# Causal masks of three forgetting pairs written into the forget terms instead of added by matmuls

## What is computed

```python
cum = lax.cumsum(log_f, axis=2)                       # one term for each head and position
logits = einsum('bhqd,bhkd->bhqk', qb, k) * scale
logits = logits + cum_q[..., :, None] - cum[..., None, :]
causal = key_pos[None, :] <= q_pos[:, None]
p = softmax(where(causal, logits, -inf), axis=-1)
out = einsum('bhqk,bhkd->bhqd', p, v)
```

## Time and profile before

| | |
|---|---|
| runs | 756.1 us median of 3 (752.18 to 759.27) |
| profiled execution | 752.78 us |
| its span, first to last instruction | 751.0 us |
| mean granted TensorE clock | 0.988 |
| TensorE busy | 704.8 us, 94% |
| VectorE busy | 490.6 us, 65% |
| ScalarE busy | 425.1 us, 57% |
| GpSimd busy | 363.0 us, 48% |

### The profile page before, as it was taken

How to read it: one execution, slowest core, us unless ns; L and a number is a source line. 1 busy time by engine, 2 the same in 40 slices (tenths; PEclk the granted TensorE clock), 3 DMA queues, 4 the chain that set the end, 5 groups by cost and what they waited for, 6 DMA issues and landing times.

```text
span 751.0 us, 10774 instructions
## 1 busy us (share of the span) xinstructions
PE 704.8 (94%) x3830; PEld 587.1 (78%) x3830; DVE 490.6 (65%) x994; ACT 425.1 (57%) x884; POOL 363.0 (48%) x300
## 2 busy tenths in 40 slices
PE   2989979899999989999999999999989999999995
PEld 0667867788888878888887788888878887888884
DVE  4977997746655776566558764655686654555566
ACT  5875656655675645566756464666565665323222
POOL 1010462466885545688757355866574653321100
PEclk9999999999999999999999999999999998999998
DMA  9932230233442110234420102445312087792222
GB/s 353 409 140 85 92 127 7 86 98 113 139 152 95 38 57 0 99 113 142 168 101 26 42 1 85 154 166 169 101 49 85 22 281 237 231 301 85 85 113 112
DMA packets 35463, 93.14 MB, mean 124 GB/s; under 512 B 4297, under 2 KB 5961, under 8 KB 34898
## 3 DMA queue, kind: packets, MB, share of 16 engines
q1 hardware_dynamic: 28450, 73.71, 28.3%
q0 software_dynamic: 5376, 14.68, 6.1%
q10 hardware_dynamic: 1584, 4.05, 1.4%
HBM read 68.81 MB, written 23.63 MB: 123 GB/s over the span
## 4 chain that ended last, share of the span: by engine, by line
PE 79%; ACT 8%; DVE 8%; issue 3%; POOL 2%; DMA 0%; DVEq 0%; ACTq 0%; POOLq 0%
PE psum L1643 12%; PE psum L1550 12%; PE psum L1552 11%; PE psum L1551 11%; PE psum L1631 8%; PE psum L1607 7%; PE psum L1576 4%; PE psum L1575 4%; DVE work L1203 2%; DVE stacks L1171 2%; PE psum L1480 1%; ACT work L891 1%; ACT work L892 1%; PE psum L1481 1%; PE psum L1494 1%
## 5 line engine op out<-in xcount | busy, mean ns | idle before, releaser
L1550 PE MATMUL psum<-h_hi,w_hi 128*128 128x512 f32 x448 | 186.4, 416 | 5.1 <-DVE stacks L1171 5.1
L1552 PE MATMUL psum<-h_hi,w_lo 128*128 128x512 f32 x448 | 176.5, 394 | 0.0
L1551 PE MATMUL psum<-h_lo,w_hi 128*128 128x512 f32 x448 | 175.4, 391 | 0.0
L686 POOL TENSOR_TENSOR work<-work 128x127 f32<-128x127 f32 (+3 forms) x64 | 80.1, 1252 | 173.3 <-DVE work L1203 173.3
L931 ACT ACTIVATE pt_hi<-psum 128x512 fp32r<-128x512 f32 (+1 forms) x192 | 87.8, 490 | 105.4 <-PE psum L1607 102.3
L1264 DVE TENSOR_TENSOR pt_lo<-psum,pt_hi 128x512 fp32r<-128x512 f32 (+1 forms) x192 | 101.0, 553 | 54.7 <-ACT pt_hi L931 52.4
L1203 DVE TENSOR_TENSOR_SCAN work<-work 128x128 f32<-128x128 f32 (+3 forms) x64 | 100.4, 1569 | 37.9 <-ACT work L892 37.7
L1550 PEld LDWEIGHTS psum<-h_hi,w_hi 128*128 128x128 f32 x448 | 85.3, 190 | 20.6 <-issue 6.5
L1552 PEld LDWEIGHTS psum<-h_hi,w_lo 128*128 128x128 f32 x448 | 84.5, 189 | 19.5
L1551 PEld LDWEIGHTS psum<-h_lo,w_hi 128*128 128x128 f32 x448 | 85.2, 190 | 14.7
L1607 PE MATMUL psum<-ident,work 128*128 128x128 f32 x576 | 88.5, 281 | 8.6 <-POOL work L686 8.0
(11 more groups left out here) (185 smaller groups left out, 1325.1 us busy)
## 6 DMA issues: line engine op xcount, KB each, us to landing
w_raw<-in_w_blocks SPq DMA_DIRECT2D x30, 512.0 KB, 4.3
w_split_scratch<-work SPq DMA_DIRECT2D x16, 512.0 KB, 3.2
work<-in_x SPq DMA_DIRECT2D x12, 512.0 KB, 7.3
work<-in_w_ada_t SPq DMA_DIRECT2D x10, 512.0 KB, 6.4
y_split_scratch<-work SPq DMA_DIRECT2D x10, 512.0 KB, 3.6
v_stack_early<-in_w_ada_t SPq DMA_DIRECT2D x8, 512.0 KB, 3.4
work<-forget_scratch SPq DMA_DIRECT2D x8, 512.0 KB, 5.1
work<-in_w_out SPq DMA_DIRECT2D x16, 256.0 KB, 3.3
```

The source lines that it names most:

```text
L1550: nc.tensor.matmul(bank, hi, h_hi[:, c_, cols], start=(c_ == 0), stop=False)
L1551: nc.tensor.matmul(bank, hi, h_lo[:, c_, cols], start=False, stop=False)
L1552: last = nc.tensor.matmul(bank, lo, h_hi[:, c_, cols], start=False, stop=(c_ == DC - 1))
```

## The change

In pairs 1, 3 and 5 the mask matmul at L1579 is left out. The mask goes into `CUM[a]` instead: GpSimd writes -1e30 above the diagonal into each of its eight 128-column blocks by one affine select in place. A unit needs its diagonal block masked and the blocks before it unmasked, so as soon as a unit is past its maximum, the block that was its diagonal one is loaded again from `c_dram`, unmasked, by a transfer that ScalarE issues behind the exponential (64 KB, none after the last unit of a head). VectorE waits for the select ahead of a head's first unit, and for the transfer ahead of each later one. GpSimd masks head 0's terms at step 13 of the stick-breaking pair before, ahead of that step's probabilities, and head 1's terms at step 2 of the forgetting pair. Pair 7 and the stick-breaking pairs keep the mask matmul.

```diff
+    def on_pe(g):
+        return is_sb(g) or g // STEPS == PAIRS - 1
+    MASK_AT = (STEPS - 3, 2)
 # GpSimd
+            def mask_forget_terms(p, a):
+                pool.wait_ge(s_cumb, 32 * (p // 2 + 1))
+                terms = CUM[a].rearrange("p (b k) -> p b k", k=P)
+                nc.gpsimd.affine_select(out=terms, in_=terms, compare_op=ALU.is_ge, fill=MASKED, base=0,
+                                        pattern=[[0, TB], [-1, P]], channel_multiplier=1).then_inc(s_cmask, 1)
...
             for g in range(UNITS):
                 p, i = g // STEPS, g % STEPS
+                if is_sb(g) and i == MASK_AT[0] and p + 1 < LAST:
+                    mask_forget_terms(p + 1, 0)
                 if g + 1 < UNITS and not is_sb(g + 1):
                     fx_probs(g + 1)
+                if not is_sb(g) and i == MASK_AT[1] and p < LAST:
+                    mask_forget_terms(p, 1)
                 if g + 2 < UNITS and is_sb(g + 2):
                     sb_probs(g + 2)
 # ScalarE, behind the exponential of unit g
+                    p, a, qb = unit(g)
+                    if qb + 1 < TB and not on_pe(g):
+                        cols = slice(qb * P, (qb + 1) * P)
+                        act.dma_start(CUM[a][:, cols],
+                                      c_dram[p - 1 + a:p + a, cols].partition_broadcast(P)).then_inc(s_cback, 16)
 # VectorE, ahead of the reduction of unit g
-                if g % TB == 0:
-                    dve.wait_ge(s_cumb, 32 * (g // (2 * STEPS) + 1))
+                p, a, qb = unit(g)
+                head = 2 * (p // 2) + a
+                if on_pe(g):
+                    if qb == 0:
+                        dve.wait_ge(s_cumb, 32 * (p // 2 + 1))
+                elif qb == 0:
+                    dve.wait_ge(s_cmask, head + 1)
+                else:
+                    dve.wait_ge(s_cback, 16 * (head * (TB - 1) + qb))
 # TensorE
                     last = nc.tensor.matmul(bank[:, 0:c1 - c0], q, stacks[:, p % 2, a, 2, c0:c1], start=False,
-                                            stop=not diagonal)
-                    if diagonal:
+                                            stop=not (diagonal and on_pe(g)))
+                    if diagonal and on_pe(g):
                         last = nc.tensor.matmul(bank[:, c1 - c0 - P:c1 - c0], ident_bf[:],
                                                 mask_bf[:, 0 if is_sb(g) else 1, :], start=False, stop=True)
```

More of the change, by code:

```diff
@@ L300, in hybrid_trunk_kernel @@
         s_cumb = sem("s_cumb")
+        s_cmask = sem("s_cmask")
+        s_cback = sem("s_cback")
         s_score = sem("s_score")
```

## The result

The changed kernel took 760.84 us (median of 20 runs, 755.57 to 767.66), the kernel before 755.88 (20 runs, 752.1 to 759.82). The ratio is 1.0055, with a 95% interval of 1.0035 to 1.0074. So the change costs about half a per cent, 4 to 5 us (0.55% is 4.2 us, the medians lie 5.0 apart), where the forecast was 0.8. The profiled execution says the same: its span is 755.2 us against 751.0, so 4.2 us longer.

The account below looks back on a forecast made before the run. TensorE, busy 704.8 of 751.0 us, was taken as the bound, with GpSimd finishing level at the last stick-breaking unit. -4.0 + 4.8 + 0 + 0 = +0.8 us gave 753.6 us (757 on the median), range 751 to 763.

Parts of the forecast that it names:

- the 1%: Whole kernel: a time within about 1% (7.5 us) of no change, which a measurement cannot tell apart; chance 0.83.
- rival (b): Unit hand-overs of pairs 1, 3, 5: restoring transfers land late, past 3.1 us, giving 761 to 778 us; chance 0.08.
- Mask products: TensorE, pairs 1, 3, 5: 42 removed masks count, 0.12 us each in even units, 0.07 in odd; 4.0 us gained.
- Head 0's select: GpSimd, last stick-breaking unit before pairs 1, 3, 5: 1.6 us each, delaying TensorE's transposes; 4.8 us lost, 3.0 to 6.9.
- my lower end: GpSimd's select of 128x1024: shortest duration assumed, 1.0 us, from the memset's slope of 0.83 ns a column.
- Head 1's select: GpSimd, step 2 of the forgetting pair: 0.8 us of delay against 3.7 us of room, so no cost.
- Restoring transfers: ScalarE's queue, pairs 1, 3, 5: 42 transfers land in 2.0 to 2.8 us; under 3.1 us they cost nothing.
- Rival (a): TensorE behind the three select stalls: 1.9 us stands drop its clock to half, giving 759 to 762 us; chance 0.17.
- Rival (c): GpSimd, first three selects: 6 us each instead of 1.6, +14 us, 770 us; chance 0.03.
- Rival (d): Last stick-breaking unit: select doesn't delay transposes or takes only 1.0 us; -1.0 to -4.6 us, 751.5 to 755; chance 0.12.
- What would show it: Expected trace signs: 80 mask products, three selects with TensorE waits of 1.5 to 2.2 us, forgetting pairs 1.3 us shorter each.

Follow-up runs that it names:

- e3: The kernel before without the 48 mask products of pairs 1, 3 and 5 and with nothing in their place; ratio 0.996.
- e9: The changed kernel with head 0's select at step 12 and without restoring transfers or their waits, blocks staying masked; ratio 0.9959.
- e5: The changed kernel with each restoring transfer reading 128 different rows of the identity matrix instead of one row 128 times, results wrong; ratio 1.0007.
- e10: The changed kernel with head 0's select at step 12 and restores reading 128 separate DRAM rows, filled before by six 512 KB transfers; computes everything; ratio 0.9964.
- e1: The changed kernel without the 42 restoring transfers and VectorE's waits for them, diagonal blocks staying masked; ratio 1.0017.
- e4: The changed kernel with the 42 transfers going into a tile nobody reads and VectorE waiting for none, blocks staying masked; ratio 1.0038.
- e6: The changed kernel with the wait for restored blocks 4 to 6 ahead of a unit's second reduction instead of the first; ratio 1.0048.
- e8: The changed kernel with head 0's select at step 12 and each block transferred one unit ahead into a spare tile, then copied by VectorE; ratio 1.0032.
- e11: As e8, but ScalarE copies the staged blocks behind its exponential and waits for the transfers in VectorE's place; ratio 0.9984.
- e12: As e10, with the wait for blocks 4 to 6 ahead of the second reduction instead of the first; ratio 0.9954, median 752.91 us.
- e2: The changed kernel with head 0's select one step earlier, at step 12 instead of 13, in GpSimd's idle time; ratio 1.0033.

## Why the prediction was right and where not

The time lies in the range and within the 1% that had most of the chance. It even lies in the forecast's own 753 to 761, but by luck: what happened is a select cheaper than assumed and rival (b), which had 0.08. The size is off: +0.8 forecast, +4.2 measured in the spans. By its steps:

- **Mask products, -4.0.** Measured -3.5 (e3, e9). The odd units' 0.07 us holds: in e3 the transposes follow the scores at the scores' own pace. The even units give 0.09, not 0.12: the term that I took from the earlier trace rows, 0.20 - 0.12 = 0.08 for the second value product, came from one row, and summed over pair 1's seven such units the value products' spacings fell by 0.39 us in e3, so 0.056 each; with the mask's own 0.04 that is 0.09.
- **Head 0's select, +4.8.** Place and path were right: three of them between split and product, each straight out as a wait of TensorE. The size was not: 1.09 us in place of 1.6, and 3.2 us in all. The slope of the memset, my lower end (1.0 us), was the better guide; the assumption that a select has more to do in a column than a memset failed. From 128 to 1024 columns it is (1.09 - 0.28) / 896 = 0.90 ns a column against 0.83 for the memset.
- **Head 1's select, 0.** Right: e9, which has it, is as short as e3, which has not.
- **Restoring transfers, 0.** This step failed, by 4.2 us, in its landing and in its path. The landing was put at 2.0 to 2.8 us from one load of equal size, which reads 128 different rows, while the 512 KB broadcast from the same scratch stood beside it with 5.1. What I named as speaking for rival (b), 128 reads of one row, is what e5 and e10 showed to be the cause. So the true minimum was the top of my bracket; what made single landings as long as 4.6 us, no run shows. The path was said to go through the score bank only, with 3.1 us of room. But the score bank carried 0.4 us. VectorE was busy enough that a wait of up to 0.9 us made its next operands late, the projection's low parts and the value blocks, and that carried 2.8 us (pairs 1, 3 and 5 against e1). The rest was a third path, which the prediction left out: these transfers make SP's weight block of pair 5 late, 1.0 us here and 1.4 in e4.
- **Rival (a), the clock.** Not seen in the changed kernel. Behind the wait at 155.48 the granted clock was 1.00, and so it was behind the other two selects. Behind longer stands it did come: in e6 and e8 TensorE stood 2.5 and 2.3 us ahead of L1643 and L1654 in pair 5, and 3.4 us at half clock begin as that stand ends, where no kernel with a shorter stand has any; but in e11 it stood 2.4 us there and the clock stayed full. The 1.26 us stand of the earlier trace rows, behind which the clock stayed full, was no safe bound: in e1, e3 and e12 the same stand is followed by half clock within 2 us, at a further stand of 0.7 us.
- **Rival (b).** This is what happened, at its near edge. Its price for landings of 3.5 us, 1.4 us a pair and 4.2 in all, is what was measured (1.5, 1.1 and 1.6), and its 761 is the median. That is luck as well: the median landing was 3.0, and the price was worked out for the score bank, which carried little.
- **Rival (c), a select that is expensive where it is called.** Not seen: six selects between other work, 1.09 to 1.11 us, with no gap before them. The Trainium skill (GPSIMD Engine Reference, § 2.1 Instruction dispatch) speaks of about 6 us at the first call into freshly loaded code; for these six calls the trace shows none.
- **Rival (d).** Its half about the lower end came true (-4.0 + 3.2 = -0.8); the restores turned it into a loss.
- **What would show it.** 80 products, the three selects and the waits before L1641 were there, 1.0 us in place of 1.5 to 2.2. Pairs 1, 3 and 5 being 1.3 us shorter each was not.

What stays open in part: why the weight block of pair 5, and hardly that of pair 1 or 3, comes late beside the restores. The timelines of SP's queue show two things. In pair 5 SP issues the block behind its jobs on `y_scratch`, where pairs 1 and 3 have jobs on `in_w_out`, and it goes out later: 55.9 us into the stage in e1, e3, e5 and e9, 56.6 to 59.1 us in every kernel where GpSimd waits over 2 us for it, while pairs 1 and 3 issue theirs at 54.2 to 55.9. And it takes longer to land, 4.7 to 6.7 us against 4.4 to 4.8. GpSimd's wait was 1.4 us in e5, whose transfers all read the same 64 KB, and 2.1 and 3.1 us in e12 and e10, whose rows are spread over 3 MB; whether that is the source or only the moment, no run separates.

## What to carry to other kernels

A transfer's landing is estimated from one that reads its source in the same way, not from one of the same size; a broadcast of one row is its own case, and the longest landings are to be held against the room, not only the middle. The room is to be read for every result that the waiting engine still has to deliver, not for the next one alone: here the next one carried 0.4 us of 3.2. When a value must be put back between two uses, ask first what the wait meets in the worst phase: in e2's profiled execution moving the select into idle time freed 3.2 us and lost 4.0, with landings of up to 5.6 us. Judge such edits by stage lengths, which repeat to 0.1 us, where medians over a clock that wanders tell half a per cent, and count the half-clock stretches of every stage before comparing it.

## What the runs showed of the hardware

- 64 KB as one 512 B row read 128 times: 2.8 us at the least, 2.9 to 3.0 in the median, up to 6.1 (e8). As 128 separate rows: 1.7 to 1.8 at the least, 1.9 to 2.0 in the median, up to 4.6 (e12).
- VectorE's copy of 128x128 fp32 between SBUF tiles: 0.22 us undisturbed, 0.60 in the median of 42 and up to 2.2 beside GpSimd (e8); ScalarE's copy of the same tiles: 0.29 us in the mean (e11).
- GpSimd's affine select of 128x1024 fp32: 1.09 to 1.11 us in six calls.
